# Value pages as 64 rows of 1 KB and sampled states as rows of 2 to 4 KB in a one-core decoder step

## The reference

```python
# group A, gated delta rule, 8 heads x 128, per sample and head: state S is 128 x 128
S = S * exp(g);  u = beta * (v - S^T k);  S = S + k u^T;  o = S^T q
# group B, block-sparse softmax attention, 8 heads x 128, over a paged pool of keys and values
past_k = k_pool[page_table].reshape(B, -1, H_MOBA, HEAD_DIM)     # pages of 128 positions, 2048 past
gate = q . mean(k of each block of 256);  keep the 3 best past blocks and the own one
p = softmax(scores + rel_bias);  o = p @ v
```

## Time and profile before

| | |
|---|---|
| median of three runs | 1587.6 us |
| profiled execution, first to last instruction (span) | 1585.7 us |
| granted clock, mean | 0.994 |
| TensorE busy | 1536.9 us, 97% |
| DVE / ACT / POOL busy | 59% / 41% / 11% |
| chain of waits, by engine | PE 79%, SP's queue 10%, DVE 4% |
| SP's queue at L602 in that chain | 5% |
| DMA packets | 105636, 365.18 MB |
| of these under 2 KB | 48650 |
| page transfers L602, SP and POOL | 192 and 192, 64 KB each |
| states before the delta rule, L674 | 16, 256 KB each |
| states in the feed-forward stage, L841 and L853 | 8 and 8, 512 KB each |

### The profile page before, as it was taken

One profiled execution on the slowest core, in us unless ns is written; L12 is line 12 of the kernel. 1 busy time (PEld: TensorE's weight loads), 2 busy tenths in 40 slices (PEclk: granted clock), 3 DMA queues, 4 the chain that ended last, 5 costly groups with the idle time before them and its releaser, 6 DMA issues.

```text
span 1585.7 us, 36205 instructions
## 1 busy us (share of the span) xinstructions
PE 1536.9 (97%) x14680; PEld 1492.7 (94%) x14680; DVE 935.0 (59%) x1139; ACT 645.6 (41%) x757; POOL 181.8 (11%) x287
## 2 busy tenths in 40 slices
PE   7999999999999799999999999999999999999996
PEld 7899999999899689998899999999999999999995
DVE  4445645557754356774586666666666644445566
ACT  5344343342524453474543333543333333333344
POOL 0000202011677400101000000000001000000000
PEclk9999999999999999999999999999999999999998
DMA  8788879786899975756645455556677555555453
GB/s 285 267 335 329 318 282 345 279 309 231 260 249 255 285 293 201 288 183 239 213 160 186 171 175 184 183 174 214 237 251 265 205 180 176 183 185 185 159 179 115
DMA packets 105636, 365.18 MB, mean 230 GB/s; under 512 B 14529, under 2 KB 48650, under 8 KB 78634
## 3 DMA queue, kind: packets, MB, share of 16 engines
q1 hardware_dynamic: 90834, 322.66, 58.4%
q0 software_dynamic: 12896, 39.73, 7.3%
q10 hardware_dynamic: 1792, 1.20, 0.4%
HBM read 353.27 MB, written 10.47 MB: 229 GB/s over the span
## 4 chain that ended last, share of the span: by engine, by line
PE 79%; SPq 10%; DVE 4%; issue 3%; ACT 2%; DMA 2%; ACTq 0%; DVEq 0%
PE psum_g L517 22%; PE psum_g L518 22%; PE psum_g L519 22%; SPq L602 5%; PE M L2152 3%; PE M L2167 3%; SPq L634 2%; DVE wl L501 2%; PE M L517 1%; PE psum_g L2461 1%; PE M L518 1%; PE M L519 1%; ACT wh L496 1%; SPq L674 1%; DMA raw<-w_in_t 1%
## 5 line engine op out<-in xcount | busy, mean ns | idle before, releaser
L517 PE MATMUL psum_g<-xh,wh 128*128 128x264 f32 (+1 forms) x2382 | 696.8, 293 | 8.5 <-DVE wl L501 5.0
L501 DVE TENSOR_TENSOR wl<-raw,wh 128x2048 fp32r<-128x2048 f32 (+1 forms) x221 | 499.3, 2259 | 305.9 <-ACT wh L496 305.0
L518 PE MATMUL psum_g<-xl,wh 128*128 128x264 f32 (+1 forms) x2382 | 677.7, 285 | 0.0
L519 PE MATMUL psum_g<-xh,wl 128*128 128x264 f32 (+1 forms) x2382 | 677.1, 284 | 0.0
L496 ACT CAST wh<-raw 128x2048 fp32r<-128x2048 f32 (+1 forms) x221 | 414.5, 1876 | 253.6 <-PE psum_g L519 205.2
L517 PEld LDWEIGHTS psum_g<-xh,wh 128*128 128x128 f32 x2382 | 450.4, 189 | 23.1 <-issue 15.2
L518 PEld LDWEIGHTS psum_g<-xl,wh 128*128 128x128 f32 x2382 | 450.8, 189 | 3.1 <-issue 2.9
L519 PEld LDWEIGHTS psum_g<-xh,wl 128*128 128x128 f32 x2382 | 449.0, 188 | 0.0
L517 PE MATMUL psum_g<-gh,wh 128*128 128x264 f32 x704 | 200.3, 285 | 0.3 <-DVE wl L501 0.2
L518 PE MATMUL psum_g<-gl,wh 128*128 128x264 f32 x704 | 199.4, 283 | 0.0
L519 PE MATMUL psum_g<-gh,wl 128*128 128x264 f32 x704 | 199.4, 283 | 0.0
(11 more groups left out here) (443 smaller groups left out, 1758.9 us busy)
## 6 DMA issues: line engine op xcount, KB each, us to landing
raw<-w_t SPq DMA_DIRECT2D x88, 1024.0 KB, 4.8
raw<-w_in_t SPq DMA_DIRECT2D x53, 1024.0 KB, 7.6
kring<-cache_k_t SPq DMA_DIRECT2D x96, 512.0 KB, 5.0
sraw<-cache_k_t SPq DMA_DIRECT2D x32, 512.0 KB, 6.5
raw<-w_out_t SPq DMA_DIRECT2D x16, 1024.0 KB, 4.9
raw<-w2a_t SPq DMA_DIRECT2D x16, 1024.0 KB, 4.8
raw<-w2b_t SPq DMA_DIRECT2D x16, 1024.0 KB, 4.8
raw<-w2c_t SPq DMA_DIRECT2D x16, 768.0 KB, 4.2
```

The source lines that it names most:

```text
L501: eng.tensor_tensor(wl[:, u % 2, 0:nk], raw[:, u % 2, 0:nk], wh[:, u % 2, 0:nk].bitcast(F32), ALU.subtract).then_inc(raw_used, 1)
L517: nc.tensor.matmul(out, hi_w, x_hi(k), start=(k == order[0]), stop=False)
L518: nc.tensor.matmul(out, hi_w, x_lo(k), start=False, stop=False)
L519: last = nc.tensor.matmul(out, lo_w, x_hi(k), start=False, stop=(k == order[-1]))
```

## The change

Host code lays two inputs out in another order, and the kernel reads them in it. `cache_v_t` has, for a page and head, 64 rows of two successive positions (1 KB), so that a page of one head is one run of 64 KB in memory. Page t of a head's six now goes to 64 of the 128 partitions (the lower for even t, the upper for odd t) and there to two neighbouring column blocks of the slot; a slot holds the same positions as before in another order. The six transposes take every second column of the probabilities to match. `state_dn_t` has the key dimension ahead of the heads, so a DMA of four heads has 128 rows of 2 KB, and one of eight heads 128 rows of 4 KB. The output of the sampled states is laid out in the same way and turned back on the host. Number, order and engine of the DMAs, semaphores and products are the same.

```diff
@@ load_values
-                    eng.dma_start(v_pages[s][:, t], a["cache_v"][0, ds(pages[6 * n_ + t], 1), :, h].rearrange("a t d -> t (a d)"))\
-                       .then_inc(v_full[s], 16)
+                    rows = slice(64 * (t % 2), 64 * (t % 2) + 64)
+                    eng.dma_start(v_pages[s][rows, t - t % 2:t - t % 2 + 2].rearrange("p s n -> p (s n)"),
+                                  a["cache_v_t"][ds(pages[6 * n_ + t], 1), h].rearrange("a p n -> p (a n)")).then_inc(v_full[s], 16)
@@ load_states, SP
-                        sp.dma_start(state_half(b, s), a["state_dn"][0, b, 4 * s:4 * s + 4].rearrange("h d e -> d h e"))\
+                        sp.dma_start(state_half(b, s), a["state_dn_t"][b, :, 4 * s:4 * s + 4])\
@@ load_state and store, POOL
-                pool.dma_start(state[:, s], a["state_dn"][0, b].rearrange("h d e -> d h e")).then_inc(h_in[s], 16)
+                pool.dma_start(state[:, s], a["state_dn_t"][b]).then_inc(h_in[s], 16)
-                pool.dma_start(o["dn_sample"][0, b].rearrange("h d e -> d h e"), state[:, s]).then_inc(h_out[s], 16)
+                pool.dma_start(o["dn_sample"][b], state[:, s]).then_inc(h_out[s], 16)
@@ beside, TensorE
                         for t in range(6):
-                            last = nc.tensor.transpose(M[:, 0, t * 64:(t + 1) * 64], probs[:, t * P:(t + 1) * P], ident[0:64, 0:64])
+                            keys_ = 256 * (t // 2) + t % 2
+                            last = nc.tensor.transpose(M[:, 0, t * 64:(t + 1) * 64], probs[:, keys_:keys_ + 255:2], ident[0:64, 0:64])
@@ laid_out
+    a["cache_v_t"] = np.ascontiguousarray(inputs["cache_v"][0].transpose(0, 2, 1, 3)).reshape(-1, H, PAGE // 2, 2 * P)
+    a["state_dn_t"] = np.ascontiguousarray(inputs["state_dn"][0].transpose(0, 2, 1, 3))
@@ returned
-            kv[1][None, SEQ:, None], mem[0][None, None], mem[1][None, None], o["dn_prompt"], o["dn_sample"],
+            kv[1][None, SEQ:, None], mem[0][None, None], mem[1][None, None], o["dn_prompt"],
+            np.ascontiguousarray(o["dn_sample"].transpose(0, 2, 1, 3))[None],
```

More of the change, by code:

```diff
@@ L594, in load_values @@
             _, pages = nc.values_load_multi_w_load_instructions(
-                pid_row[:, at:at + 6 * len(heads)], engines={kind}, min_val=0, max_val=a["cache_v"].shape[1] - 1,
+                pid_row[:, at:at + 6 * len(heads)], engines={kind}, min_val=0, max_val=a["cache_v_t"].shape[0] - 1,
                 skip_runtime_bounds_check_because="each value is an entry of the page table")
@@ L2563, in _ @@
             last_square(2, [xt[:, 1]])
-_PLAIN = ["cache_v", "state_dn", "state_conv", "page_table", "dn_a_log",
+_PLAIN = ["state_conv", "page_table", "dn_a_log",
           "dn_dt_bias", "dn_norm_w", "rel_bias"]
 _OUT = [("y", (P, KC, T)), ("kv", (P, 2 * H, T)), ("mem_k", (P, HX, N_MEM)), ("mem_v", (P, 2, HX * P)),
-        ("dn_prompt", (1, 1, H, P, P)), ("dn_sample", (1, NSAMP, H, P, P)),
+        ("dn_prompt", (1, 1, H, P, P)), ("dn_sample", (NSAMP, P, H, P)),
         ("edge", (P, 24, 3 + NSAMP)), ("conv_kept", (NSAMP, CONV_W - 2, 24 * P))]
```

## The result

The changed kernel is slower: a median of 1603.5 us over four runs (1600.7 to 1605.6), beside 1588.1 us for the kernel before. The measured ratio of the two kernels is 1.0083, with a 95% interval of 1.0066 to 1.0101; the two medians alone would give 1.0097. I had forecast 1579.6 us, so the sign is wrong and the time lies outside the range. TensorE's waits from 500 to 600 us sum to 21.7 us; over 8 was my sign of being wrong in the main.

A forecast was written before the change was run, and what follows sets the result against it. It took the values stretch to be limited by pieces, not bytes, with SP using up its lead. Values 3.0, state wait 3.3, clock 1.4 and L1635 1.1 made 8.8 us, less 0.8 for new waits: 1579.6 us, range 1575.5 to 1585.5.

The forecast's parts named there:

- my sign of being wrong in the main: TensorE's waits from 500 to 600 us, 12.5 us before the change, still summing to over 8 us.
- SP's issue price: Values stretch: each of SP's 192 page issues falls from 333 ns to 0.31 us, 4 us off SP's queue.
- Pushing back goes: Values stretch: with less backlog, SP's prolonged issues (up to 1.3 us) mostly go, worth at most 12 us to SP.
- A 1 KB piece: Values stretch, SP's queue: 50 ns per 1 KB piece against 32 ns for 512 B, lowering the share to about 0.85.
- POOL: Values stretch: POOL's page issues each take 25 ns less, 0.3 us a group, so its last pages start some 2 us earlier.
- States before the delta rule: SP's 16 state issues fall to 333 ns; the 3.3 us state wait goes, and 1.1 us at L1635 is won.
- Clock: After the state wait, 552 to 556 us: the slow spell at 0.65 goes with the wait, winning 1.4 us.
- Transposes: Values: six transposes reading every second column of the probabilities cost 0, at most 1.3 us more.
- Feed-forward stage: State loads and stores there win 0, bounds -0.5 and +0.5 us; POOL's load issues fall from 882 ns towards 535.
- The range: Whole kernel: 1575.5 us with all waits gone but the hand-over's, to 1585.5 us with POOL pacing and unchanged issues.
- The slower rival: Values stretch: 1 KB pieces to half the partitions take 93 ns, stretch 11 us longer, 1593.6 us; chance 0.10.
- Rival four: SP's issues don't shorten; only the state wait shrinks, by some 2.7 us, and its slow spell goes: 1583.5 us; chance 0.09.

The follow-up runs named there:

- e_rows128: The changed kernel, but each page of a head moved as 128 rows of 512 B, with the old transposes; 0.9970 of the kernel before, median 1586.0 us.
- e_states: The kernel before with only the states' layout changed, pages as before; 0.998 of the kernel before, 3 us faster.
- e_pool64: The changed kernel, but both of SP's heads moved as 128 rows of 512 B, only POOL's two keeping 64 rows of 1 KB; 0.9976 of the kernel before.
- e_48rows: The changed kernel, but only the first 48 of each page's 64 rows moved; 0.9960 of the kernel before, median 1584.7 us.

## Why the prediction was wrong

- *SP's issue price.* This step failed and carried the sign. I set 0.31 us between 294 ns for 16 rows and 333 ns for 128, as if the price rose with the rows. Measured: 0.469 us. The trace had no 64-row transfer; I wrote so, but for the issue I took the neighbours as bounds. "4 us off" was 26 us on. I had named SP's queue as the pace of the stretch, and that was right: it is why 136 ns on each issue became 13 us.
- *Pushing back goes.* It shrank from 17.7 to 7.6 us and could not pay for the dearer issues. Part of that is only that SP fed less: in `e_rows128`, with issues of 333 ns, it is 17.9 us.
- *A 1 KB piece.* I took 50 ns. By the same working, 50.1% of 139 us by 16 is 1114 us; less eight weight loads (385 us) 729 us remain for some 170 pages of 64 pieces, 67 ns. That is two 512 B pieces of 32 ns: under load the larger piece wins nothing. The packets themselves, from 440 to 540 us, took 31.6 ns in the mean for 512 B before and 62.9 for 1 KB now. So my reading of the earlier trace rows, that the stretch is limited by pieces and not by bytes, doesn't hold between these two sizes. The share fell from 0.92 to 0.89 because SP fed less, while POOL's queue took more for its bytes. The rows behind it, from 401 to 540 us: SP's queue now, POOL's before and now:

```profile
q1 hardware_dynamic: 14670, 19.47, 50.1%
```

```profile
q0 software_dynamic: 6368, 13.91, 33.2%
```

```profile
q0 software_dynamic: 6287, 13.73, 36.0%
```

- *POOL.* I took 25 ns off each issue; it is 13 ns (535 to 522). I had also halved the pieces of all 384 page transfers; the packets of POOL's queue stayed the same in number.
- *States before the delta rule.* The term was too large: I had summed 5.8 us for the wait, the clock and L1635, and `e_states` is 3 us faster (1 to 6 by its interval). Issues cost 432 ns and not 333, and the states come into use only 1.1 to 1.6 us sooner after their first issue. The rest of the wait hung on SP being early, and there the working stands: with the first state issue at 534.3 us in `e_pool64` and at 533.7 in `e_48rows`, the wait is gone; with it at 541.4 in `e_rows128` 2.4 us stay, within the 1 to 3 that I had put for that case. In the changed kernel 2.1 us stay.
- *Clock.* In the changed kernel the granted clock is 0.84 from 540 to 560 us and 0.98 from 440 to 540: three spells at the lower level instead of one, as shown under the result. They came with the page waits instead of going. In `e_pool64`, with no wait over 2 us before the hand-over, it is 1.00 in both windows and TensorE has no wait for the states.
- *Transposes.* Taken as free. They went from 224 to 280 ns in the median and their weight loads from 140 to 219, with first to last start 0.6 us instead of 0.4. Small, as bounded. Weight loads before, then both now:

```profile
L2340 PEld LDWEIGHTS M<-C,pj x6: 136/140/142, 421.8 to 422.1; 64*128 64x128 f32 x6
```

```profile
L2342 PEld LDWEIGHTS M<-C,pj x6: 192/219/220, 420.9 to 421.5; 64*128 64x128 f32 x6
L2342 PE MATMUL M<-C,pj x6: 280/280/329, 420.9 to 421.5; 64*128 64x64 f32 x6
```

- *Feed-forward stage.* Taken as nothing. The issues of POOL's loads fell from 882 to 528 ns, and TensorE's busy time from 980 to 1260 us stayed the same: right.
- *The range.* Its lower end takes 1.7 us for the clock, where the sum has 1.4, without a row for the difference, and 1587.6 less 12.0 is 1575.6, not 1575.5. Neither matters here.
- *Rivals.* The slower rival had the sign and the place right and the mechanism wrong, so its 1593.6 us is nearer by luck. It asked for a DMA share of 0.95 or more, and the share was 0.89. It took 93 ns for a piece; 67 came out, below the 78 from which it was to decide. `e_pool64` shows its effect, 2.4 us of page waits, without a loss in time. Rival four, issues that don't shorten, was one step from the truth: I let them stay at 333 ns and didn't let them lengthen. The rule on partition halves, in the Trainium skill's "DMA: Bandwidth & Descriptors", section "Rules for kernel authors", asks for one transfer to 128 partitions because both halves share the same transfer engines. These runs agree with its advice: `e_pool64` (0.9976) gains nothing over `e_rows128` (0.9970). What decided here is another thing, SP's price of an issue.

## What to carry to other kernels

Where a queue's issues pace a stretch, the price of one issue is a term of its own; measure it for the new shape before counting on fewer or larger pieces, and don't interpolate it between two shapes. Bytes, pieces and issues are three separate budgets: this change took away 18432 of 105636 packets, left the bytes, and lost on the issues. Multiply each uncertain nanosecond by its count and see from which value the sign turns: here some 40 ns on each of 192 issues, if all of them arrive, would have eaten the forecast of 8 us.

## What the runs showed of the hardware

- SP's issue of a transfer of exactly 64 rows takes 592 to 598 ns back to back against 420 to 432 for the seven other multiples of 16 up to 128. It does so for rows of 256 B to 2 KB, in the lower half, the upper half or from row 32, in one run or 4 KB apart. With register work ahead it is 469 against 333. POOL's does not show it (526 ns, between 539 at 128 rows and 487 at 16). Why 64 is special no run here tells; nor was ACT's queue tried.
- Issues that follow at once cost SP 432 ns; with about 0.19 us of other work between, 333. So an issue's recorded duration depends on what stands before it. The step from one issue to the next is no shorter for it: 0.526 us in the pages, 0.46 back to back.
- Reading with a step of two columns, TensorE's weight load of 64 rows by 128 columns of float32 took 219 ns instead of 140 (six loads in each kernel).
- Transfers to 64 partitions from POOL beside transfers to 128 from SP (`e_pool64`): the landing of the latter is 6.0 us in the median against 3.5 before, and the share of the transfer engines 1.10 against 0.92, for 272 and 259 GB/s. With 64 rows from both (the changed kernel) the landing is 3.7 us and the share 0.89, at 240 GB/s; there SP issues more slowly, which may be why. Why transfers to halves do this no run here tells.
- 512 B and 1 KB pieces on SP's queue took 31.6 and 62.9 ns in the mean beside the other traffic of 440 to 540 us.
